# Sparse attention: eight items of a chunk taken in the order of query tiles 3, 0, 3, 0, 2, 1, 2, 1 instead of rising

## The reference, cut to what matters

```python
s = jnp.einsum('bgrqd,bgkd->bgrqk', qc, kw, preferred_element_type=f32)
s = s - sl * dist_w.astype(f32)
p = masked_softmax(s, m_w)
o_win = jnp.einsum('bgrqk,bgkd->bgrqd', p.astype(dt), vw)
...
o = (gc[0][..., None] * o_cmp.astype(f32) + gc[1][..., None] * o_sel.astype(f32)
     + gc[2][..., None] * o_win.astype(f32)).astype(dt)
```

## Time and profile before

| what | us |
|---|---|
| median of 3 runs | 3472.15 |
| the runs | 3468.49 to 3474.07 |
| span of the profiled execution | 3465.9 |
| TensorE busy in it | 3383.6 (98%) |
| VectorE busy | 1657.3 (48%) |
| ScalarE busy | 1174.3 (34%) |

### The profile page before, as it was taken

The page is one execution under the profiler, slowest core; times in us unless marked ns, Lnnn a source line. Parts: engine busy times, 40 slices in busy tenths (PEclk is TensorE's granted clock), DMA queues, the critical chain, the costliest instruction groups (busy, mean ns, idle before and its releaser), DMA issues. The chain is left out here.

```text
span 3465.9 us, 43643 instructions
## 1 busy us (share of the span) xinstructions
PE 3383.6 (98%) x16822; PEld 2334.1 (67%) x16822; DVE 1657.3 (48%) x2802; ACT 1174.3 (34%) x1864; POOL 27.7 (1%) x24
## 2 busy tenths in 40 slices
PE   8999999999999999999999999999999999999998
PEld 6788888866788887757886444436757887444435
DVE  7765544468665636776334111117767334111116
ACT  5632223247522224365333100005356333000004
POOL 0000000000000000000001000000000001000000
PEclk9999999999999999999999999999999999999999
DMA  4322222220122222221228999993230226999994
GB/s 162 101 92 96 97 97 97 97 100 2 49 96 95 96 95 67 85 80 47 96 89 307 406 420 420 420 419 127 80 101 31 92 96 262 393 420 420 420 420 169
DMA packets 123870, 628.69 MB, mean 181 GB/s; under 512 B 13948, under 2 KB 14980, under 8 KB 76872
## 3 DMA queue, kind: packets, MB, share of 16 engines
q1 hardware_dynamic: 123720, 626.63, 47.6%
HBM read 621.25 MB, written 7.42 MB: 181 GB/s over the span
## 5 line engine op out<-in xcount | busy, mean ns | idle before, releaser
L458 PE MATMUL PS<-WK_r,RING_r 128*128 128x512 f32 x1312 | 511.9, 390 | 0.0
L456 PE MATMUL PS<-WK_r 128*128 128x512 f32 x856 | 336.2, 393 | 0.0
L457 PE MATMUL PS<-HT_r,WK_r 128*128 128x512 f32 x856 | 333.8, 390 | 0.0
L458 PEld LDWEIGHTS PS<-WK_r,RING_r 128*128 128x128 f32 x1312 | 245.4, 187 | 53.9
L450 ACT ACTIVATE WK_r<-RING 128x1024 fp32r<-128x1024 f32 x126 | 133.1, 1058 | 384.2 <-PE PS L458 375.7
L458 PE MATMUL PS<-AR_r,RING_r 128*128 128x512 f32 x624 | 242.7, 389 | 0.0
L456 PE MATMUL PS<-AR_r,RING_r 128*128 128x512 f32 x624 | 242.7, 389 | 0.0
L453 DVE TENSOR_TENSOR RING_r<-RING,WK_r 128x1024 fp32r<-128x1024 f32 x126 | 154.4, 1227 | 178.5 <-ACT WK_r L450 178.5
L453 DVE TENSOR_TENSOR RING_r<-RING,RING_r 128x1280 fp32r<-128x1280 f32 (+1 forms) x80 | 112.8, 1411 | 244.5 <-ACT RING_r L450 244.4
L453 DVE TENSOR_TENSOR RING_r<-RING,EXTRA_r 128x1024 fp32r<-128x1024 f32 x136 | 165.7, 1219 | 94.7 <-ACT EXTRA_r L450 94.7
L456 PE MATMUL PS<-EXTRA_r 128*128 128x512 f32 x528 | 205.8, 390 | 1.4 <-DVE RING_r L453 1.3
(11 more groups left out here) (505 smaller groups left out, 6085.8 us busy)
## 6 DMA issues: line engine op xcount, KB each, us to landing
AR<-moe SPq DMA_DIRECT2D x144, 1024.0 KB, 22.6
RING<-moe SPq DMA_DIRECT2D x120, 1024.0 KB, 21.0
EXTRA<-moe SPq DMA_DIRECT2D x72, 1024.0 KB, 19.9
RING<-ff_in SPq DMA_DIRECT2D x96, 512.0 KB, 3.3
RING<-branch SPq DMA_DIRECT2D x64, 640.0 KB, 3.9
RING<-ff_out SPq DMA_DIRECT2D x48, 512.0 KB, 3.3
WK<-moe SPq DMA_DIRECT2D x24, 1024.0 KB, 24.3
RING<-mix_in SPq DMA_DIRECT2D x44, 512.0 KB, 3.3
```

Source lines behind the costliest of these rows:

```text
L456: nc.tensor.matmul(out, r(w_high), r(x_high), start=start, stop=False)
L457: nc.tensor.matmul(out, r(w_high), r(x_low), start=False, stop=False)
L458: return nc.tensor.matmul(out, r(w_low), r(x_high), start=False, stop=stop)
```

## The change

The eight items that follow the compressed one in each chunk are taken in another order. Before, it was tile 0 selected, tile 0 window, tile 1 selected, tile 1 window, and so on up to tile 3. After, a list names tile and branch for the positions 1 to 8. Each item's own instructions, the compressed item's place, the pipeline's order of steps, the buffers and the places of `output` and of the conversions (by number n) stay as they are.

```diff
             halves = [slice(0, 64), slice(64, 128)]
+            BLOCKS = [(3, 1), (0, 1), (3, 2), (0, 2), (2, 1), (1, 1), (2, 2), (1, 2)]
 
             def place(n):
 
                 c, k = divmod(n, STEP)
-                return c, k == 0, (k - 1) // 2, 1 + (k - 1) % 2
+                return c, k == 0, *BLOCKS[k - 1]
```

## The result

The new order is slower, by about 0.4%. Four executions took 3488.53 us in the median (3481.89 to 3496.68) against 3470.36 for four of before (3468.49 to 3474.07): a ratio of 1.0042, 95% interval 1.0027 to 1.0056. A later measurement with six more executions, beside 21 of before, gave 3488.05 against 3471.67, ratio 1.0048 (1.0033 to 1.0063). The profiled execution of the changed kernel has a span of 3480.1 us and took 3481.89, the fastest of the ten. Time and span differ by 1.7 to 1.9 us in every execution that has both, so of the 6.25 us by which the median of before stands above its profiled span some 4.4 are a difference between executions, and not what lies before the first and behind the last instruction.

What follows compares the result with a forecast made beforehand. PE was taken to set the pace, busy 19.68 of 20.13 us a chunk. The ring's 1.37 us more a chunk, 11.0 in eight, plus 0.2 for the ends gave 3472.15 + 11.2, about 3483; forecast 3479.1 to 3489, range 3476 to 3489.

Steps and rivals of the forecast that it cites:

- The ring: Changed stage: closed loop of waiting steps from `turn` of position 1 to the next chunk's, 21.50 us against 20.13.
- steps 11 and 12: Next chunk: wide `score` and `shift` until DVE's next step, 2.40 us; then compressed `weigh` until its `turn`, 1.37.
- step 3: On ACT: `output` of the chunk before, standing behind the copy of position 1, 0.48 us.
- longer ring: Another loop the rows can't exclude: 0.5 us a chunk more gives +15.2 (3487.4); its sign, a chunk of 22 or more.
- The waits: PE's waits grow from 0.45 to about 1.8 us a chunk, before `turn` of positions 0 (compressed), 3 and 4.
- The ends: Once each: first chunk's wide `score` +0.6 us, shorter last item -1.2, conversions 0.8; together +0.2.
- the 0.8 taken for all of them: Conversions behind the copies of n = 55 and n = 64: bounds 0 and 1.7 us, 0.8 taken.
- the rival of a fall in each chunk: PE's clock falls once in each chunk: 8 x 1.7 = 13.6 us added to the 11.2, 3497; chance 0.08.
- 1.7 us a fall: Full speed lost while PE stood at 1.2 GHz, read elsewhere in the earlier trace after 3 us only 1.56 busy.
- the last of the list of signs: In the trace after, all stages before and behind the changed one would be as they were.
- The clock rival: Same as the rival of a fall in each chunk: 3497 us, chance 0.08.

Runs made afterwards that it cites:

- the two orders that interleave wide and narrow items most: The new order (3488.53 us, ratio 1.0042), and the new order's list changed to tiles 0, 3, 0, 3, 2, 1, 2, 1 (3484.32 us, ratio 1.0038).
- the falling order: Only the list of tiles differs: 3, 3, 2, 2, 1, 1, 0, 0, equal neighbours, widest behind the compressed item; 3483.18 us, ratio 1.0028 to before.

## Why the prediction was right, and where it was short

**The ring.** Its sum of 21.50 us is the chunk that was measured, and the steps hold one by one: predicted and measured are 1.13 and 1.13, 0.92 and 0.93, 0.48 and 0.47, 1.54 and 1.55, 1.26 and 1.26, 1.13 and 1.13, 1.17 and 1.17, 1.38 and 1.36, 2.92 and 2.91, 3.79 and 3.80, 3.77 and 3.78 (steps 11 and 12 together), 2.01 and 2.01. That it is this ring that bounds, and not only one that happens to fit, is shown by taking step 3 out of it: 0.49 us went, and the same edit in the rising order brought nothing. No longer ring was missed.

**The waits.** About 1.8 us a chunk was predicted, with 0.8 in front of `turn` p0, then p3 and a small one at p4; the rows have 0.84, 0.55, 0.20, and 0.19 at p6, which hadn't been named: 1.78.

**The ends.** +0.2 was predicted on top of 11.0; without a fall of the clock the stage was longer by 10.9. The conversions cost 1.6 us in the one period where they can be read apart (23.13 against 21.50), where before it was 0.6 (20.72 against 20.12): more than the 0.8 taken for all of them, and the other ends made up for it.

**Interleaving and the clock.** PE leads in the busy times of the chunk, and the two orders that interleave wide and narrow items most lost 1.3 to 1.4 us in each. The Trainium skill (Perfetto Trace Analysis, section Optimization Strategy) says that interleaving may help where the most-contended engine changes over time. By the busy times of the chunk it is PE in either order, so these runs don't test that; they show that interleaving can cost where one engine leads. The clock fell once in this stage, in one of the two profiles of the new order, in the last chunk, where the conversions stretch PE's wait to 1.61 us (the other profile has that wait and no fall); in the regular chunks, with waits of 0.84 us and less, it stood at 1.00 in both. So the rival of a fall in each chunk is out. Its price, 1.7 us a fall, was read at a fall that cost no time: that of the earlier trace rows is the one that PE's next wait took in. The Trainium skill (TensorE: Matmul & The Clock Gate, section A second HAM failure mode: psum-queue depth-cycling) tells of short idle times between groups of products that made a kernel's clock swing. Such waits were there, and in the regular chunks they cost only their own length.

**What was short.** The time was 3488.5 us and not 3483, 5.5 us above the value. That it is inside the range, by half a microsecond, is luck: the upper end was set for a longer ring, and no such ring came. The step that failed is the last of the list of signs, that all stages before and behind would be as they were. Their work is, to 0.01 us in the stretches behind the stage where the clock is full; but their falls of the clock came at other places, and the two that were looked at behind the stage, where PE set the pace, cost 1.6 us each. The sum had no term for it. At the same mean clock the new order was 12.3 us slower, near the 11.2 of the sum. The clock rival had the right kind of cost in the wrong place: it looked for it in the waits of the changed stage.

## What to carry to other kernels

In a pipeline whose order is written out on several in-order engines, look for the closed ring of steps (a semaphore's wait or a place in an engine's list) that comes back one period later, and add up its hand-overs from rows of the present trace: the sum is a floor for the period, and here it was the period to 0.01 us in an order that had never run. Balanced busy times say nothing about it; items that stand side by side should differ little in size, so that each one's hand-overs fit under its neighbours' work; in the falling order it was the compressed item and the tile 3 behind it that differed. Read such a change in its own stage first, since a few us more or less come from the clock elsewhere.

## What the runs showed of the hardware that was not expected

What a fall of TensorE's clock to half costs hangs on what PE was doing just then: in two stretches with the same instructions and one fall each (mean 0.96 both), one took 40.00 and the other 41.63 us, and the cheaper fall lay ahead of a wait of PE. Over ten executions of one kernel the time ran from 3481.9 to 3496.8 us with the mean clock from 0.995 to 0.990, so nearly all of its spread goes with the clock. And a product of two 128 by 128 float32 tiles with weights loaded for each costs PE 0.22 us (50 of them 11.2), a transpose of the same size 0.11 (eight blocks 1.02, four 0.58).
